# A hybrid decoder layer on one Trainium2 core: the first two projections side by side, tile of x by tile of x

## The reference

```python
h = rms_norm(x, norm_mix[l])
(hq, hf, hi, hg, nq, kc, vc, ksl, vsl, kwn, vwn, ngate, gate_a, gate_b) = jnp.split(h @ w_in[l], offsets, axis=-1)
y_a = hgrn2_mixer(hq, hf, hi, hg, lower_bounds[l], hg_out_gain[l]) @ w_branch_a[l]
y_b = nsa_mixer(nq, kc, vc, ksl, vsl, kwn, vwn, ngate, ...) @ w_branch_b[l]
mixed = jax.nn.sigmoid(gate_a) * y_a + jax.nn.sigmoid(gate_b) * y_b
x = x + mixed @ w_out[l]
h = rms_norm(x, norm_mlp[l])
x = x + jnp.square(jax.nn.relu(h @ w_up[l])) @ w_down[l]
```

## Time and profile before

| | |
|---|---|
| runs | 805.68, 806.44, 806.84 us; median 806.44 |
| the profiled execution | 806.03 us; its span 804.3, so 1.7 us lie around the span |
| busy of the span | PE 99%, PEld 79%, POOL 61%, DVE 49%, ACT 24% |
| the chain that ended last | 96% PE, then ACT, POOL, DMA and DVE with about 1% each |
| DMA | 78 MB, 97 GB/s over the span; 283 GB/s in the first 20 us |

### The profile page before, as it was taken

How to read it: one execution, slowest core, us unless ns; L and a number is a source line. 1 busy time by engine, 2 the same in 40 slices (tenths; PEclk the granted TensorE clock), 3 DMA queues, 4 the chain that set the end, 5 groups by cost and what they waited for, 6 DMA issues and landing times.

```text
span 804.3 us, 12357 instructions
## 1 busy us (share of the span) xinstructions
PE 797.1 (99%) x4632; PEld 635.8 (79%) x4632; DVE 396.2 (49%) x565; ACT 196.3 (24%) x402; POOL 489.1 (61%) x325
## 2 busy tenths in 40 slices
PE   9999999999999999999999999999999999999998
PEld 7788878988787666577888888888888888888886
DVE  5794577734465445633457667661000476650000
ACT  6101753214311445725112222220000122210000
POOL 5666544676454755555666566676666676676663
PEclk9999999999999999999999999999999999999999
DMA  8244222233522010015223223233223223323320
GB/s 282 98 139 154 82 80 80 79 106 105 183 79 78 27 53 28 1 53 183 84 101 104 89 95 104 80 102 105 84 99 104 82 102 104 98 85 131 130 78 26
DMA packets 23549, 78.01 MB, mean 97 GB/s; under 512 B 2723, under 2 KB 3499, under 8 KB 23380
## 3 DMA queue, kind: packets, MB, share of 16 engines
q1 hardware_dynamic: 19964, 69.00, 25.8%
q10 hardware_dynamic: 3544, 8.44, 2.9%
HBM read 75.31 MB, written 4.21 MB: 99 GB/s over the span
## 4 chain that ended last, share of the span: by engine, by line
PE 96%; ACT 1%; POOL 1%; DMA 1%; DVE 1%; issue 0%; SPq 0%; DVEq 0%; POOLq 0%; ACTq 0%
PE bank L385 27%; PE bank L387 26%; PE bank L386 26%; PE bank L709 3%; PE bank L731 3%; PE bank L752 2%; PE bank L467 1%; PE bank L468 1%; PE bank L469 1%; PE bank L409 1%; ACT gates L1081 1%; PE bank L516 1%; DMA x<-in_xT 1%; POOL wsp L305 1%; PE bank L625 1%; PE bank L741 1%
## 5 line engine op out<-in xcount | busy, mean ns | idle before, releaser
L305 POOL TENSOR_TENSOR wsp<-wraw,wsp 128x1024 fp32r<-128x1024 f32 x124 | 305.8, 2466 | 10.3
L303 POOL TENSOR_SCALAR wsp<-wraw 128x1024 fp32r<-128x1024 f32 x124 | 135.3, 1091 | 243.7 <-PE bank L387 159.2
L385 PE MATMUL bank<-hhi,wsp 128*128 128x512 f32 x352 | 140.6, 399 | 0.9 <-POOL wsp L305 0.4
L386 PE MATMUL bank<-hlo,wsp 128*128 128x512 f32 x352 | 137.3, 390 | 0.0
L387 PE MATMUL bank<-hhi,wsp 128*128 128x512 f32 x352 | 137.3, 390 | 0.0
L385 PE MATMUL bank<-ghi,wsp 128*128 128x512 f32 x256 | 100.4, 392 | 0.0
L387 PE MATMUL bank<-ghi,wsp 128*128 128x512 f32 x256 | 99.7, 389 | 0.0
L385 PE MATMUL bank<-uhi,wsp 128*128 128x512 f32 x256 | 99.7, 389 | 0.0
L386 PE MATMUL bank<-glo,wsp 128*128 128x512 f32 x256 | 99.6, 389 | 0.0
L386 PE MATMUL bank<-ulo,wsp 128*128 128x512 f32 x256 | 99.6, 389 | 0.0
L387 PE MATMUL bank<-uhi,wsp 128*128 128x512 f32 x256 | 99.6, 389 | 0.0
(11 more groups left out here) (246 smaller groups left out, 1012.1 us busy)
## 6 DMA issues: line engine op xcount, KB each, us to landing
wraw<-in_w SPq DMA_DIRECT2D x126, 512.0 KB, 3.3
bias_skewed<-bias_lines ACTq DMA_DIRECT2D x1, 2048.0 KB
bias<-bias_skewed ACTq DMA_DIRECT2D x1, 2048.0 KB, 8.7
x<-in_xT ACTq DMA_DIRECT2D x1, 2048.0 KB, 8.1
out<-x ACTq DMA_DIRECT2D x8, 256.0 KB, 2.0
x<-in_xT SPq DMA_DIRECT2D x3, 512.0 KB, 6.6
x<-in_xT SPq DMA_DIRECT2D x2, 256.0 KB, 4.4
wraw<-in_w SPq DMA_DIRECT2D x4, 128.0 KB, 8.0
```

Source lines behind the costliest of these rows:

```text
L303: pool.tensor_scalar(whi[:, two, :], wraw[:, raw, :], 1.0, 0.0, ALU.mult, ALU.add).then_inc(w_hi, 1)
L305: pool.tensor_tensor(wlo[:, two, :], wraw[:, raw, :], whi[:, two, :].bitcast(F32), ALU.subtract).then_inc(w_split, 1)
L385: pe.matmul(out_, wh, mh, start=first, stop=False)
L386: pe.matmul(out_, wh, ml, start=False, stop=False)
```

## The change

The first two projections become one loop over the tiles of x (`first_two`): for each tile three matmuls of chunk 0 into bank 0, then three of chunk 1 into bank 1. Both chunks are loaded in halves that stand between the parts of x in SP's queue. GpSimd now splits chunk 0 in quarters and takes the low quarters of chunk 1 between them; ScalarE makes the high quarters of chunk 1 between the tiles of x. Chunks 2 and 3 get split slots of their own (`w23`, 16 KB per partition), so neither waits for the use of an earlier chunk; chunks 4 and 5 then take the two old slots and wait for the use of chunks 0 and 1. Of the warm-up matmuls 9 are left.

```diff
-WARM = 16
+WARM = 9
+FIRST_ORDER = ["x0", "w00", "x1", "w10", "x2", "w01", "w11", "x3", "x4"]
...
+        w23 = at("w23", 128.5, [P, 2, 2, CW], F32R)
...
-            load(0, 0)
-            for n, (a, b) in enumerate(X_PARTS):
-                sp.dma_start(x0[:, a:b, :], xT[:, a:b, :]).then_inc(x_in[n], 16)
-            for n in range(4):
-                q = slice(256 * n, 256 * n + 256)
-                sp.dma_start(wraw[:, 1, q], w[1, :, q]).then_inc(w1_in[n], 16)
+            for part in FIRST_ORDER:
+                n = int(part[-1])
+                if part[0] == "x":
+                    a, b = X_PARTS[n]
+                    sp.dma_start(x0[:, a:b, :], xT[:, a:b, :]).then_inc(x_in[n], 16)
+                else:
+                    c, h = int(part[1]), slice(512 * n, 512 * n + 512)
+                    sp.dma_start(wraw[:, c, h], w[c, :, h]).then_inc(w01_in[c][n], 16)
...
+            def quarter_low(c, n, done):
+                q = slice(256 * n, 256 * n + 256)
+                pool.tensor_tensor(wlo[:, c, q], wraw[:, c, q], whi[:, c, q].bitcast(F32), ALU.subtract).then_inc(done, 1)
+
             for half in range(2):
+                pool.wait_ge(w01_in[0][half], 16)
+                for n in (2 * half, 2 * half + 1):
+                    q = slice(256 * n, 256 * n + 256)
+                    pool.tensor_scalar(whi[:, 0, q], wraw[:, 0, q], 1.0, 0.0, ALU.mult, ALU.add).then_inc(w0_hi, 1)
+                    pool.wait_ge(w0_hi, n + 1)
+                    quarter_low(0, n, w0_lo)
+                for n in (2 * half, 2 * half + 1):
+                    pool.wait_ge(w1_hi, n + 1)
+                    quarter_low(1, n, w1_lo)
+            pool.wait_ge(w0_lo, 4)
             pool.wait_ge(w1_lo, 4)
-            pool.sem_inc(w_hi, 1)
-            pool.sem_inc(w_split, 1)
+            pool.sem_inc(w_hi, 2)
+            pool.sem_inc(w_split, 2)
             pool.wait_ge(w2_hi, 1)
             pool.sem_inc(w_hi, 1)
-            pool.tensor_tensor(wlo[:, 0, :], wraw[:, 2, :], whi[:, 0, :].bitcast(F32), ALU.subtract).then_inc(w_split, 1)
-            for c in range(3, AT["gb2"] + 1):
+            pool.tensor_tensor(w23[:, 1, 0, :], wraw[:, 2, :], w23[:, 0, 0, :].bitcast(F32), ALU.subtract).then_inc(w_split, 1)
+            pool.wait_ge(w_landed[3], 16)
+            pool.tensor_scalar(w23[:, 0, 1, :], wraw[:, 3, :], 1.0, 0.0, ALU.mult, ALU.add).then_inc(w_hi, 1)
+            pool.wait_ge(w_hi, 4)
+            pool.tensor_tensor(w23[:, 1, 1, :], wraw[:, 3, :], w23[:, 0, 1, :].bitcast(F32), ALU.subtract).then_inc(w_split, 1)
+            for c in (4, 5):
+                pool.wait_ge(w_landed[c % NRAW], 16)
+                pool.wait_ge(w_used, c - 3)
+                split(c, c % NRAW, c % NSPLIT)
+            for c in range(6, AT["gb2"] + 1):
                 split_straight(c)
...
+            def first_two(each_k):
+                for k in range(KT):
+                    each_k(k)
+                    c = slice(k * P, k * P + P)
+                    for n, low in enumerate((w0_lo, w1_lo)):
+                        if k % 2 == 0:
+                            pe.wait_ge(low, k // 2 + 1)
+                        last = three(bank[n][:], whi[:, n, c], wlo[:, n, c], hhi[:, k, :], hlo[:, k, :], k == 0,
+                                     k == KT - 1)
+                        if k == KT - 1:
+                            last.then_inc(w_used, 1)
...
-            first_projection(0, x_split)
-            first_projection(1, w_quarter)
+            first_two(x_split)
...
+            x_high(0)
+            x_high(1)
+            w1_high(0)
+            x_high(2)
+            w1_high(1)
+            x_high(3)
+            x_high(4)
             act.wait_ge(w_landed[2], 16)
-            act.wait_ge(w_used, 1)
-            act.activation(whi[:, 0, :], wraw[:, 2, :], ACT.Copy).then_inc(w2_hi, 1)
+            act.activation(w23[:, 0, 0, :], wraw[:, 2, :], ACT.Copy).then_inc(w2_hi, 1)
```

More of the change, by code:

```diff
@@ L188, in build_block @@
         x_in = [sem(f"x_in{n}") for n in range(len(X_PARTS))]
-        w1_in = [sem(f"w1_in{n}") for n in range(4)]
+        w01_in = [[sem(f"w{c}{n}_in") for n in range(2)] for c in range(2)]
+        w0_hi, w0_lo = sem("w0_hi"), sem("w0_lo")
         w1_hi, w1_lo, w2_hi = sem("w1_hi"), sem("w1_lo"), sem("w2_hi")
@@ L208, in build_block @@
         x_hi, x_lo, h_hi = sem("x_hi"), sem("x_lo"), sem("h_hi")
-        half_split = sem("half_split")
         tok_stat, tok_rs = sem("tok_stat"), sem("tok_rs")
@@ L308, in split_straight @@
             def split_straight(c):
-                pool.wait_ge(w_landed[c % NRAW], 16 * (c // NRAW + (c % NRAW != 1)))
+                pool.wait_ge(w_landed[c % NRAW], 16 * (c // NRAW + (c % NRAW > 1)))
                 if c >= NSPLIT:
@@ L322, in _ @@
-            pool.wait_ge(half_split, 4)
-            pool.sem_inc(w_hi, 1)
-            pool.sem_inc(w_split, 1)
[L325 to L329, removed]
+                pool.wait_ge(w01_in[0][half], 16)
[4 more added lines that the diff above has]
+                    quarter_low(0, n, w0_lo)
@@ L361, in _ @@
                     c = POOL_FIRST + j
-                    pool.wait_ge(w_landed[c % NRAW], 16 * i + 16 * (c // NRAW + (c % NRAW != 1)))
+                    pool.wait_ge(w_landed[c % NRAW], 16 * i + 16 * (c // NRAW + (c % NRAW > 1)))
                     pool.wait_ge(w_used, 4 * i + (c - NSPLIT + 1))
@@ L409, in stat @@
                 pe.matmul(to[:, 0:n], matrix, squares, start=True, stop=True).then_inc(stat_out, 1)
+            def first_two(each_k):
[9 more added lines that the diff above has]
+                            last.then_inc(w_used, 1)
             def first_projection(n, each_k):
-                if n < 2:
-                    wh, wl = whi[:, n, :], wlo[:, n, :]
-                else:
-                    wh, wl = take(CHUNKS[n])
+                pe.wait_ge(w_split, n + 1)
+                wh, wl = w23[:, 0, n - 2, :], w23[:, 1, n - 2, :]
                 for k in range(KT):
@@ L885, in _, with x_high, w1_high @@
             act.wait_ge(small_landed, 16)
-            for n, (a, b) in enumerate(X_PARTS):
+            def x_high(n):
                 act.wait_ge(x_in[n], 16)
-                for k in range(a, b):
+                for k in range(*X_PARTS[n]):
                     act.activation(hhi[:, k, :], x0[:, k, :], ACT.Copy, scale=g_mix[:, k:k + 1]).then_inc(x_hi, 1)
-            for n in range(4):
-                q = slice(256 * n, 256 * n + 256)
-                act.wait_ge(w1_in[n], 16)
-                act.activation(whi[:, 1, q], wraw[:, 1, q], ACT.Copy).then_inc(w1_hi, 1)
+            def w1_high(half):
+                act.wait_ge(w01_in[1][half], 16)
+                for n in (2 * half, 2 * half + 1):
+                    q = slice(256 * n, 256 * n + 256)
+                    act.activation(whi[:, 1, q], wraw[:, 1, q], ACT.Copy).then_inc(w1_hi, 1)
+            x_high(0)
[5 more added lines that the diff above has]
+            x_high(4)
             act.wait_ge(w_landed[2], 16)
-            act.wait_ge(w_used, 1)
-            act.activation(whi[:, 0, :], wraw[:, 2, :], ACT.Copy).then_inc(w2_hi, 1)
+            act.activation(w23[:, 0, 0, :], wraw[:, 2, :], ACT.Copy).then_inc(w2_hi, 1)
             for n in range(4):
```

14 lines of the change are left out of this document (removed).

## The result

| | before | after |
|---|---|---|
| median of the runs | 806.31 us (805.68 to 806.84, 8 runs) | 808.35 us (807.32 to 808.61, 8 runs) |
| profiled execution, span | 806.03, 804.3 | 807.85, 806.1 |

The ratio is 1.0025, with a 95% interval of 1.0014 to 1.0036: the change costs 2.0 us. I had forecast 805.5 and a range up to 807.9. The time lies beyond the range, on the side of the rival that I had given 0.2.

A forecast was written before the change was run, and what follows sets the result against it. TensorE, busy 99% of the span, was taken as the bound, its late first matmul at 8.11 as the loss. 1.1 gained less 0.2 waiting gave 0.9: 805.1 profiled, 805.5 as median; range 804.3 to 807.9 for 8 in 10.

The forecast's parts named there:

- The rival of the slow clock: First two projections: pauses at 5.3-6.0 and 7-8.2 keep TensorE's clock low until 14.2; +1.9, 808.3 us; chance 0.2.
- from 8.2 the other 45 take 45 x 0.228 = 10.3 us: First two projections: after 3 of 48 matmuls, the rest run at 0.228 us each, if nothing is late.
- The clock's own term: Slow-clock rival, from 8.2: each us at half rate costs half a us; a rise at 14.2 loses 3.0 on 1.1 gained.
- The steady start, 8.2: Front: TensorE starts at about 6.0, then stands until 8.2 for chunk 1's first low quarter, done at 8.15.
- the forecast's gain of 1.1: End of the second projection: 18.5 against 19.63 before, 1.1 us gained.
- by bytes ahead at 4.3: SP's queue: transfers placed by bytes ahead; chunk 0's first half and tile 0 together arrive at 4.3.
- The end of the second projection: Second projection: steady start 8.2 plus 10.3 us for 45 matmuls ends at 18.5, against 19.63 before.
- The places I gave for the later tiles and quarters: First two projections: later low parts and quarters ready at 9.5 to 15.5; tile 4 tightest, ready and needed at 13.0.
- The sums as a cap: Fourth projection: sums of squares ready at 26.8 to 26.9, reached at 26.7; TensorE waits 0.2, capping the gain.
- Slots: zero: Third projection onward: earlier splits of chunks 2 and 3 and later reloads bring TensorE zero.
- Everything behind moves as one piece: Behind the sums of squares: chains hang on TensorE or keep their slack, so the rest moves as one piece.

The follow-up runs named there:

- The second execution: The changed kernel with its 9 warm-up matmuls, executed once more for a second trace with nothing altered: 808.32 us.
- another with the same front: Changed kernel with 16 warm-up matmuls and VectorE's steps on the tables moved behind the first four results: 807.10 us, ratio 1.0011 to the kernel before.
- the pauses filled: Changed kernel with 13 warm-up matmuls and 6 more between chunk 0's and chunk 1's matmuls of tile 0: 806.32 us, ratio 0.9999 to the kernel before.

## Why the prediction was wrong, point by point

**The choice of the likeliest case.** The rival of the slow clock was named with its mechanism and, at 808.3, with the time that came. I gave it 0.2, because "the pauses are short and the last of them ends early". Nothing in the earlier trace rows said how short is short enough: they show one rise after unbroken work. All four traces with nine warm-up matmuls have lost the clock or got it late. The step that failed is "from 8.2 the other 45 take 45 x 0.228 = 10.3 us": it takes the fast clock for granted behind two pauses, by a trace in which no pause stood before the rise. In the trace after the 45 took 11.8 (9.59 to 21.38). Shown by the warm-up given back (-1.95 us) and taken from the kernel before (+1.57).

**The clock's own term.** In the first trace after, seven matmuls from 9.59 to 12.74 take 3.15 us instead of 1.6: +1.55. It was not a rise that came late, as I had drawn it, but a rise at 5.9, where the trace's record of the clock begins, just behind the warm-up, and a fall at 9.32. The second execution shows the rival as I had drawn it: the clock rises at 14.4 (I had 14.2), and 13 matmuls from 8.88 on cost 2.6 more than at the fast rate. The times, 807.85 and 808.32, are near each other because the second had its data 0.7 us earlier. Of the eight runs of the change, five have a granted clock of 0.996 to 0.998, which says that it fell; the other three have 1.000, as the second execution, and lie at 808.30 to 808.36, so the form without a fall is no exception. That my 808.3 met the median is in part luck: its two terms were 1.1 gained and 3.0 lost, and in the second execution they are 0.4 and 2.6.

**The steady start, 8.2.** It was 9.59: 1.4 us off, and this alone takes more than the forecast's gain of 1.1. Most of it, 1.2, is chunk 0's half, by bytes ahead at 4.3, which came at 5.51. From there GpSimd's pieces led to the fourth matmul in 4.1 us, where I had 3.9: each piece was 0.1 longer (0.41 and 0.74 for 0.31 and 0.64), but one turn of VectorE fell out, since tile 1 came at 7.43 and not at 5.1. The first low quarter's 1.21 is the 0.64 and the turn of 0.6 that I had counted. Over the seven traces with this queue chunk 0's half came at 4.34 to 5.51, so 4.3 was the early end, and tile 1 at 6.55 to 7.43, always late. With the clock kept P2 was 18.88 in one trace, a gain of 0.52 rather than 1.1, and 19.34 in another with the same front. The warm-up itself ended at 5.89, not at 5.3: I had taken nine sixteenths of a stretch whose end ran at the fast rate.

**The end of the second projection.** 8.2 + 10.3 = 18.5 was the sum; 9.59 + 10.3 + 1.55 is 21.4, and the trace has 21.15 + 0.23. From 12.74 on no input was late: 37 starts of 0.228 us are the 8.41 to 21.15. The places I gave for the later tiles and quarters were not put to the test, since TensorE came later than planned.

**The sums as a cap.** Forecast at 26.9 with a wait of 0.2. With the clock kept they are ready at 25.04 + 1.42 = 26.46, and asked for at 27.30: no wait. The mechanism, additions and splits in turn, is there, but the cap never bound except with the old slots (0.7 us).

**Slots: zero.** Right for the slots alone. What I had not said is that the order needs them: 3.0 us without.

**Everything behind moves as one piece.** Right for the change itself: P2 to END is 781.23 against 781.15. Wrong for an earlier front: 781.56 with 16 warm-up matmuls, 781.60 with the pauses filled. With 16 warm-up matmuls 0.2 of the 0.4 lost is the bank at 33.24. The other 0.2 I could not pin to one wait: against the kernel before, the lead shrinks in steps of 0.05 us between 85 and 377 us. The one remedy tried made it worse, and the cause stays open. VectorE's later start is a suspect that was argued, not shown.

## What to carry to other kernels

Warm-up matmuls are not idle time to be cut to the arrival of the data: before taking one away, ask what TensorE does until the first steady stretch, and fill the pauses, but only where the fill ends before the data come: at the slow clock six matmuls took 2.76 us instead of 1.50 and held the real work. A gap that stands in no trace has no price yet; give a known risk a chance by the lack of evidence against it, not by how small the gap looks. The first transfers of a kernel should be dated from traces with the same transfers in the same order, with the scatter seen there (1.2 us for chunk 0's half, 1.45 for tile 1 with whole chunks).
